# Scaling the modulation weights on ScalarE instead of GpSimd in a two-block fp32 network kernel

## The reference

```
c_act = silu(c)                                   # one vector of 1024
mod   = c_act @ mod_w[layer] + mod_b[layer]       # 6 vectors of 1024 for each of 2 layers
shift, scale = split(c_act @ kv_mod_w + kv_mod_b) # 2 more for the shared K/V
h = h + g1 * mixer(modulate(rms_norm(h), sh1, sc1))
h = h + g2 * swiglu(modulate(rms_norm(h), sh2, sc2), w_in, w_out)
```

## Time and profile before

| | |
|---|---|
| time, median of 3 runs | 2347.27 us (2342.69 to 2348.81) |
| time of the profiled execution | 2343.47 us |
| its span, first to last instruction | 2341.5 us |
| mean granted TensorE clock | 0.969 of full speed |
| TensorE matmuls busy | 2200.5 us (94%) |
| VectorE busy | 1411.5 us (60%) |
| ScalarE busy | 752.0 us (32%) |
| GpSimd busy | 424.6 us (18%) |

### The profile page before, as it was taken

One profiled execution on the slowest core, in us unless ns is written; L12 is line 12 of the kernel. 1 busy time (PEld: TensorE's weight loads), 2 busy tenths in 40 slices (PEclk: granted clock), 3 DMA queues, 4 the chain that ended last, 5 costly groups with the idle time before them and its releaser, 6 DMA issues.

```text
span 2341.5 us, 25720 instructions
## 1 busy us (share of the span) xinstructions
PE 2200.5 (94%) x10094; PEld 1760.6 (75%) x10094; DVE 1411.5 (60%) x1929; ACT 752.0 (32%) x961; POOL 424.6 (18%) x272
## 2 busy tenths in 40 slices
PE   7899999979999997999989999998999988999997
PEld 5588788757888886866778888876578776788885
DVE  5676765554766766287344444477556656655556
ACT  1443333332222223256332222244223233322321
POOL 0000000049988863010000000001410100000000
PEclk9999999989999998999999999999989998999998
DMA  6343332125555543321122322322013212323220
GB/s 248 121 157 108 102 114 73 56 89 198 188 182 188 180 162 117 117 99 64 52 75 90 108 90 92 106 93 72 18 54 108 81 63 72 108 90 108 90 90 37
DMA packets 39327, 249.54 MB, mean 107 GB/s; under 512 B 4627, under 2 KB 4819, under 8 KB 11112
## 3 DMA queue, kind: packets, MB, share of 16 engines
q1 hardware_dynamic: 32856, 230.97, 28.5%
q0 software_dynamic: 3008, 10.63, 1.4%
q10 hardware_dynamic: 3344, 6.29, 0.7%
HBM read 241.58 MB, written 6.29 MB: 106 GB/s over the span
## 4 chain that ended last, share of the span: by engine, by line
PE 80%; DVE 9%; issue 5%; POOL 3%; ACT 2%; DMA 1%; SPq 0%; ACTq 0%; DVEq 0%; POOLq 0%
PE bank L680 23%; PE bank L682 22%; PE bank L681 22%; PE bank L907 2%; DVE w_lo L1846 2%; PE bank L727 1%; ACT w_hi L1373 1%; PE bank L1025 1%; PE bank L1035 1%; PE bank L1046 1%; POOL raw L593 1%; PE bank L714 1%; DMA raw<-in_wts 1%; PE bank L823 1%; POOL raw L594 1%
## 5 line engine op out<-in xcount | busy, mean ns | idle before, releaser
L680 PE MATMUL bank<-u_hi,w_hi 128*128 128x512 f32 x1708 | 700.2, 410 | 56.5 <-DVE w_lo L1846 18.8
L681 PE MATMUL bank<-u_lo,w_hi 128*128 128x512 f32 x1708 | 676.5, 396 | 0.0
L682 PE MATMUL bank<-u_hi,w_lo 128*128 128x512 f32 x1708 | 675.8, 396 | 0.0
L1846 DVE TENSOR_TENSOR w_lo<-raw,w_hi 128x2048 fp32r<-128x2048 f32 x162 | 427.8, 2641 | 237.6 <-ACT w_hi L1373 237.5
L680 PEld LDWEIGHTS bank<-u_hi,w_hi 128*128 128x128 f32 x1708 | 328.5, 192 | 147.8 <-issue 49.3
L1373 ACT ACTIVATE w_hi<-raw 128x2048 fp32r<-128x2048 f32 x162 | 309.1, 1908 | 348.4 <-PE bank L682 306.9
L682 PEld LDWEIGHTS bank<-u_hi,w_lo 128*128 128x128 f32 x1708 | 327.3, 192 | 71.0
L681 PEld LDWEIGHTS bank<-u_lo,w_hi 128*128 128x128 f32 x1708 | 328.5, 192 | 67.7 <-issue 4.4
L680 PE MATMUL bank<-g_hi,w_hi 128*128 128x512 f32 x772 | 306.1, 396 | 13.6 <-DVE w_lo L1846 6.4
L681 PE MATMUL bank<-g_lo,w_hi 128*128 128x512 f32 x772 | 302.0, 391 | 0.0
L682 PE MATMUL bank<-g_hi,w_lo 128*128 128x512 f32 x772 | 301.7, 391 | 0.0
(11 more groups left out here) (284 smaller groups left out, 2266.4 us busy)
## 6 DMA issues: line engine op xcount, KB each, us to landing
raw<-in_wts SPq DMA_DIRECT2D x218, 1024.0 KB, 4.9
spectra<-pool ACTq DMA_DIRECT2D x16, 256.0 KB, 2.0
scr<-in_rel POOLq DMA_DIRECT2D x16, 256.0 KB, 3.2
pool<-spectra POOLq DMA_DIRECT2D x16, 256.0 KB, 3.0
H<-in_x ACTq DMA_DIRECT2D x1, 2048.0 KB, 21.1
out<-H SPq DMA_DIRECT2D x8, 256.0 KB, 2.0
pool<-in_window POOLq DMA_DIRECT2D x1, 1024.0 KB, 9.0
pool<-in_filt_w POOLq DMA_DIRECT2D x1, 512.0 KB, 6.3
```

The source lines that it names most:

```text
L680: pe.matmul(out, lh, rh, start=start, stop=False, skip_group_check=True)
L681: pe.matmul(out, lh, rl, start=False, stop=False, skip_group_check=True)
L682: return pe.matmul(out, ll, rh, start=False, stop=stop, skip_group_check=True)
L1846: dve.tensor_tensor(w_lo[RING[w]][:, :], raw[W_STREAM[w] % raw_ring][:, :], w_hi[RING[w]][:, :].bitcast(F32), ALU.subtract).then_inc(lo_do ...
```

## The change

The multiplication by the activation goes from GpSimd to ScalarE. ScalarE does it in place in `raw`, chunk by chunk, in eight activations of 128x256 with the function Identity, a scale taken from a column of `cact` and a bias taken from a column of zeros. They stand in `feed`, right behind the copy to `w_hi` of W slot w, for every M slot that stands before w in the stream. Each counts a new semaphore `m_scaled` up; GpSimd waits for all eight of its slot and then adds the halves as before.

```diff
+        m_scaled = sem("m_scaled")
...
                 for m in range(M_POOLED, NM):
                     s = M_STREAM[m]
                     src = raw[s % raw_ring]
-                    pl.wait_ge(raw_in[s % raw_ring], 16 * (s // raw_ring + 1))
-                    chunks = src[:, :].rearrange("p (k c) -> p k c", k=KC)
-                    link(pl.tensor_tensor(chunks, chunks, cact[:, :].unsqueeze(2).broadcast_to((P, KC, 256)), ALU.mult))
+                    pl.wait_ge(m_scaled, KC * (m - M_POOLED + 1))
                     link(pl.tensor_tensor(src[:, 0:1024], src[:, 0:1024], src[:, 1024:2048], ALU.add))
...
+            def scale_mod(m):
+
+                s = M_STREAM[m]
+                src = raw[s % raw_ring]
+                act.wait_ge(raw_in[s % raw_ring], 16 * (s // raw_ring + 1))
+                for k in range(KC):
+                    x = src[:, k * 256:(k + 1) * 256]
+                    act.activation(x, x, ACT.Identity, bias=zcol[:, 0:1], scale=cact[:, k:k + 1]).then_inc(m_scaled, 1)
+
             def feed(upto):
...
                     act.activation(w_hi[RING[w]][:, :], raw[s % raw_ring][:, :], ACT.Copy).then_inc(hi_done, 1)
+                    for m in range(M_POOLED, NM):
+                        if M_BEFORE[m] == w:
+                            scale_mod(m)
                     fed[0] += 1
```

## The result

The changed kernel takes 2460.19 us in the median of 4 runs (2458.58 to 2461.16); the kernel before took 2347.86 in the median of 4. The ratio is 1.0487, 95% interval 1.0472 to 1.0502. The forecast was 2463. The profiled execution took 2460.97 us with a span of 2459.1, 117.6 more than the span before.

A forecast was written before the change was run, and what follows sets the result against it. TensorE set the pace, GpSimd close behind; the change closes a 15.6 us loop against 11.50 a slot. Stage +113.7, norm -5.3, K projection +10.4 give +118.8 us on 2343.47; forecast 2463, range 2438 to 2510.

The forecast's parts named there:

- the loop: Copy W(w), scale M(w-1), GpSimd adds, SP requests W(w+1), it lands, next copy; no TensorE work in it; 15.6 us.
- The period: One pass of copy, scaling, additions, request and landing for every W slot: 15.6 us against 11.50 a slot now.
- (a): ScalarE's copy to `w_hi`, to the start of the next activation: 1.82 us.
- (b): ScalarE's eight activations of 128x256 that scale an M slot: 4.2 us, bounds 3.4 and 4.8.
- (c): GpSimd's wake-up, 0.1 us, and its three additions, 4.55 us without collision with VectorE; 6.5 with one.
- (d): From the end of GpSimd's last addition through request and landing to the next copy: 4.95 us, landing 4.8.
- The stage in time: Copies of fi2 at 517.3, fi3 at 537.5, then 28 periods to fo9 at 974.3: loss of +113.7 us.
- The norm: Norm behind the stage: GpSimd idle there, so the chain to the column sums is shorter: -5.3 us.
- The K projection: Loop runs three more times, from the copy of kk1 to that of vv0: +10.4 us.
- rival 1: Collisions persist: a GpSimd addition still waits for VectorE in each period, making it 17.5 us; 2522 us; chance 0.10.
- rival 3: The loop is hidden and the kernel faster, through relief of GpSimd: 2332 us; chance 0.03.
- rival 2: TensorE's clock becomes the bound, falling in the loop's gaps; 36 slow matmuls a slot give 2525 us; chance 0.08.

The follow-up runs named there:

- run 1: Changed kernel with the M slot ahead of W slot w scaled before the wait for W(w) and its copy, not behind: 2363.48 us, ratio 1.0081.
- run 2: Kernel before, GpSimd keeping its multiplication but first waiting for the copy to `w_hi` of the W slot behind its M slot: 2534.89 us, ratio 1.0807.
- run 7: Changed kernel with each M slot scaled one slot earlier, behind the copy of the W slot before it: 2333.34 us; with Copy without bias 2333.01.
- run 3: Changed kernel with only one of an M slot's eight activations issued, the other chunks left unscaled: 2404.89 us, ratio 1.0256.
- run 6: Kernel before with GpSimd's multiplication left out and put nowhere else, M slots unscaled: 2326.16 us, ratio 0.9920.

## Why the prediction was right, point by point

**What bounds the kernel.** That TensorE sets the pace and that the loop is the danger is shown by runs 1, 2 and 7: the same work in three places of ScalarE's order gives 2460, 2363 and 2333 us, and one wait without any moved work gives 2535.

**The period.** Forecast 15.6 us, measured 15.52. (a) 1.82 forecast; 518.38 to 520.20 is 1.82. (b) 4.2 forecast, 4.02 to 4.03 measured: 586 ns each where the row at 512 columns gave 603, 0.49 us from start to start. (c) 4.65 forecast; with its wake-up GpSimd took 0.07 + 4.58 in the first round of the chain above. No collision: `w_lo` from 540 to 860 us (min/median/max), for the earlier trace rows:

```profile
L1857 DVE TENSOR_TENSOR w_lo<-raw,w_hi x21: 2291/2292/2293, 540.2 to 851.2; 128x2048 fp32r<-128x2048 f32 x21
```

(d) 4.95 forecast, from the end of the last addition to the next copy; 4.98 and 5.04 in the rounds shown, of which the transfer is 4.95 and 5.00 (4.8 forecast). The transfers requested at 548.75 are again a pair, for the earlier trace rows:

```profile
L569 SPq DMA_DIRECT2D raw<-in_wts x2: 328/380/432, 548.8 to 549.1; - x2
...
DMA to landing us min/median/max: 4.9/6.0/7.0
```

The first round adds up to 1.82 + 4.02 + 0.07 + 4.58 + 4.98 = 15.47, so nearly all of the small error is in (b). The median of the 28 periods is 15.4; two of 16.7 and 16.9, in which a transfer took 6.19 and 6.41 us, raise the mean to 15.52. Nothing in the forecast had these, so the last 0.1 us of the agreement is luck.

The Trainium skill's page "ScalarE: Activation LUTs" (What ACT_TABLE_LOAD costs) gives figures from which one activation of (b) is estimated at 585 ns, and 93 less without the bias operand. The measured 586 and 493 agree with both, better than the 603 estimated from the rows did.

**The stage in time.** Copy of fi2 forecast for 517.3, measured 518.38; fi3 537.5 and 538.25; fo9 974.3 and 972.77. The first copy already came 1.2 us later than before. TensorE starts fo9 behind `w_lo`, at 974.72 + 2.29 = 977.0 against 864.8: +112.2 for a forecast of +113.7.

**The norm.** Forecast -5.3. The column sums in the chain, for the earlier trace rows, and VectorE's last additions, for the earlier trace rows:

```profile
1003.89 1.88 PE bank L816 x8
```

```profile
1001.11 0.68 DVE L1891 TENSOR_TENSOR scr<-scr 128x512 f32<-128x512 f32 x1
...
1002.37 1.47 DVE L1891 TENSOR_TENSOR scr<-scr 128x512 f32<-128x512 f32 x2
```

1003.89 - 896.37 = 107.5, so the norm gives back 4.7 us. No addition takes 3.43 us any more.

**The K projection.** Forecast +10.4. kk1 to vv0 takes 46.06 us, three periods of 15.35. The rest, 117.6 - 107.5 = 10.1 us, is what the span gains from the norm to the end. One detail was wrong: I had M slot 55 summed 10 us before vv2 needs it. In fact the copy of vv2, at 1081.94, waited for its transfer, while TensorE had done with vv0 at about 1064.74 + 4.2 + 10.9 = 1079.8. The two us did no harm, as TensorE had vv1 to work on.

**The base.** The sum of 118.8 was put on the profiled execution (2462), although the working says that the median of the runs lies 3.8 higher; with that the forecast would have been 2466 and not 2463. By medians the loss is 112.3 us here, and 116.8 against the 2343.42 that the kernel before took in the series of runs 1 to 3 and 6: its single executions lie between 2339 and 2349. So the 2.8 us between forecast and result are within this scatter and say little. The spans of the two profiled executions, 117.6 apart for a forecast of 118.8, are the better test.

**Busy times.** GpSimd's fell by 197 us (forecast 132 + 68). ScalarE's grew by 141, not 173: overlapping activations are counted once there, and I had added their durations. TensorE was busy 75 to 84% of a stretch and not 73%, since slow matmuls count as busy: from 540 to 970 us it did 1431 matmuls, 333 in 100 us, which is 73% of the 453 at full clock.

**The rivals.** Collisions (rival 1) did not occur, and runs 2 and 3 show what they cost where the group is too short to shield GpSimd: 1.6 to 2.1 us a period. The gain (rival 3) exists, and run 6 prices it at 17 us. The clock (rival 2) fell, to a mean of 0.88 to 0.91 in the stage, without a cost that shows. Two stretches of four microseconds in an fo slot:

```profile
568.00:572.00 4.00, 0.15 (x1) 0.00 (x0) 0.80 (x1) 2.74 (x3) 0.00 (x0) 1.00 0.70 297
...
576.00:580.00 4.00, 4.00 (x13) 3.18 (x12) 1.14 (x3) 0.00 (x0) 3.55 (x3) 0.52 0.00 0
```

TensorE stands in the middle of the slot, as forecast (its longest waits are for L1945, 58.8 us in nine). Then it runs 13 matmuls in 4 us, four of them the short ones of `macc`, where full clock gives 18 (453 in 100 us); those of 128x512 start 0.43 us apart for 0.23. Of the 1323 of that size from 540 to 970 us 144 took 0.58 us or more for 0.39, about 5 of the 48 in a slot, where the working had given 24 as free (11.5 + 24 x 0.17 is 15.6, not the 15.7 that stands there). The copies stay 15.5 us apart through it. That the clock costs nothing is read from this distance; no run here held the clock alone.

## What to carry to other kernels

Before work is moved to another engine, follow the order of that engine's queue around a ring of buffers: a step placed behind the arrival of slot w must not be what frees the buffer of slot w+1. Add the loop up (here 15.5 us) and set it against the pace of the engine that should bound; if it is longer, place the step one slot earlier before making it cheaper. And ask which instructions two engines start together: a step between them can be a shield, and taking it away can cost what it saves.

## What the runs showed of the hardware that was not expected

- In the rows read here, whichever of GpSimd and VectorE starts later waits for the other's whole instruction. That the two wait for each other was known from the kernel before; that 0.11 us decide who waits was not. `w_lo` ran its full 2.29 us while the multiplication beside it, released 0.11 us later, took 5.65 us for 3.60; in the earlier trace rows it is `w_lo` that grows, to a median of 4.15. The Trainium skill's "GPSIMD Engine Reference" (Specifications) names VectorE's instructions with two inputs from SBUF among those in contention with GpSimd, and `w_lo` and `g_lo` are of this kind. VectorE's L1945, with one input from PSUM, kept its 0.75 us beside a busy GpSimd.
- Of two 1 MB transfers requested 0.4 us apart the first keeps its 4.9 us, and the second lands after 7.0. In two of the 28 periods of the changed kernel the first took longer (6.19 us at 595.19, 6.41 at 673.48); what it met there is open.
